# Attention of an encoder on one core: the softmax pipeline rearranged over ScalarE, VectorE, GpSimd and TensorE

## The chip, the cores and the metric

The kernel runs on one core of one Trainium2 chip. The metric is device time of the whole kernel in microseconds (us). The engines are named as in the profile: PE (TensorE matmul), PEld (TensorE weight load), DVE (VectorE), ACT (ScalarE), POOL (GpSimd), SP (SyncE, which issues the loads).

## The reference, cut to what matters

A two-layer encoder over 16 + 1024 = 1040 tokens of width 1024. Layer 0 has a mixer of a Fourier part and an attention with 6 query heads and 2 key/value heads of width 128; layer 1 has a gated recurrence; each layer has an MLP of width 4096. The change lies in the attention alone:

```
s = jnp.einsum('bqhgd,bkhd->bhgqk', qb, k).astype(jnp.float32) * scale
p = jax.nn.softmax(s, axis=-1).astype(v.dtype)
o = jnp.einsum('bhgqk,bkhd->bqhgd', p, v)
```

Every query attends to all 1040 keys, in float32.

## The kernel before, in words

Float32 products are made out of three matmuls each, with both operands split in a high part (rounded to the matmul format `fp32r`) and a low part (the rest): high x high, high x low, low x high. So `qh`/`ql`, `kh`/`kl`, `pth`/`ptl`, `vth`/`vtl` are the high and low parts of queries, keys, turned probabilities and values.

The tokens are padded to T = 1044 = 9 x 116 = 3 x 348. A **tile** is 116 queries of one query head against all 1044 keys. A **group** is three tiles (348 queries) of one head, and there are 18 groups, so 54 tiles. Tile number b * 6 + s is made by `attend(b, s)`, which stands once in the stream of each engine; b runs over 0..9 (a loop for 1..8, written out for 0 and 9) and s over 0..5. Each engine runs its own copy in its own order, and semaphores tie them: `begun` and `drained` switch off the parts of a step for which no tile exists yet or any more. For tile g (numbered from 0), in `attend` number g:

- PE: nine score matmuls into PSUM banks 0, 1, 2, one bank for 348 keys (L1942). For the first tile of a group it first waits for the low part of the group's queries (`a_ql`). Before the first matmul it waits until the exponential of tile g-1 is done (`a_exp`), since that has read the three banks. Then a third of the V products of an older group (27 matmuls for a group, 9 in each step, L1956), into bank 6 or 7. Then it turns the normalized probabilities of tile g-1 (nine transposes, three for each of the banks 3, 4, 5, L1969), and before each bank it waits for the low part that was made from that bank's old content (`a_pl`).
- DVE: low part of turned third 0 of tile g-2 (L1356), then the maximum of each score bank (L1365, three), two small instructions that make the bias of the exponential (L1367, L1370), then the low parts of thirds 1 and 2, in s = 1 and 4 the low part of the next group's queries (`q_low`, L1349), and last the reciprocal of the sum (L1381), which waits for the exponential.
- ACT: the exponential of all 1044 columns with its sum (L807), the high part of turned third 0 of tile g-1 (L813), the multiplication by the reciprocal (L819), high parts 1 and 2, and at times the copy of a finished group's output (L825) or the high part of the next queries (L769).
- POOL has nothing to do here. It splits weights elsewhere (L596 makes the high part by a multiplication by a broadcast column of ones, L598 the low part by a subtraction). The split of the out projection's first unit is made before the attention, and that of its second once PE has begun the first.

Of the kernel before, what the change touches and what calls it, by code (L numbers as in the profile page):

```python
# [78 lines left out]
def encoder(nc, x, meta, mix_gain, ab_w_in, q_gain, k_gain, ab_w_out, c_w_in, lb_logits, o_gain,  # L79
# [3 lines left out]
    with ctx:  # L83
# [28 lines left out]
        nqsc = at("nqsc", [P, NQ, 9], F32, o_c + 1484 + 72 + 216)  # L112
        amax = at("amax", [P, 8], F32, o_c + 1484 + 72 + 432)
        e_c = o_c + 1484 + 72 + 432 + 32

# [20 lines left out]
        ptl = at("ptl", [P, 2, 9, CB], F32R, o_x + 9216 + 25088)  # L136
        prob = (at("prob0", [P, T], F32, o_x + 9216 + 50176), at("prob1", [P, T], F32, o_t + 9216))
        qh = at("qh", [P, 2, CB], F32R, o_x + 9216 + 50176 + row)
# [79 lines left out]

        c_sp, c_dve = sem("carrier_sp"), sem("carrier_dve")
        w_land = [sem("unit_landed0"), sem("unit_landed1")]  # L220
# [51 lines left out]
        a_nb = sem("exp_bias_ready")  # L272
        a_exp = sem("exp_done")
        a_rc = sem("sum_inverse_ready")
# [166 lines left out]

        def turned(r):
            return ps[0:TT, 3 + r, 0:3 * TT].rearrange("p (a b) -> p a b", b=TT)

# [143 lines left out]
        def _(pool):  # L588
# [12 lines left out]
            for u in range(2):  # L601
                split(u, u % 2, 16, first=True)
            with pool.Fori(1, U_DN[0] // 2) as i:
                for slot in range(2):
                    split(i * 2 + slot, slot, i * 16 + 16)
# [70 lines left out]
        def _(act):  # L676
# [120 lines left out]

            def attend(b, s):

                g = b * 6 + s  # L800
                if not drained(b, s, 0):

                    act.wait_ge(a_nb, g + 1)
                    if begun(b, s, 2):

                        act.wait_ge(a_t, b * 18 + (3 * s - 3))
# [3 lines left out]
                def high(r):  # L810
                    if begun(b, s, 1) and not drained(b, s, 1):
                        act.wait_ge(a_t, b * 18 + (3 * s - 2 + r))
                        A(tile_cols(pth, s - 1)[:, 3 * r:3 * r + 3, :], turned(r), ACT.Copy).then_inc(a_ph, 1)  # L813

                high(0)
                if not drained(b, s, 0):
# [3 lines left out]
                high(1)  # L820
                high(2)
                if s in (2, 5) and begun(b, s, 8):

                    act.wait_ge(a_pv, b * 2 + (s // 3 - 1))
                    A(yf[:, bass.ds(group_col(b - 1, s // 3), CB)], ps[:, 6 + s // 3, 0:CB], ACT.Copy).then_inc(a_ev, 1)  # L825
                if s in (0, 3) and not drained(b, s, 0):

                    q_high(b + s // 3, 1 - s // 3)

            for s in range(6):  # L830
                attend(0, s)
            with act.Fori(1, 9) as b:
                for s in range(6):
                    attend(b, s)
            for s in range(6):
                attend(9, s)

# [306 lines left out]
        def _(dve):  # L1144
# [200 lines left out]

            def q_low(b, gg):
                dve.wait_ge(a_qh, b * 2 + (gg + 1))
                nc.vector.sem_inc(c_dve, 1)
                V.tensor_tensor(ql[:, gg, :], yf[:, bass.ds(group_col(b, gg), CB)], qh[:, gg, :], ALU.subtract).then_inc(a_ql, 1)  # L1349

            def attend(b, s):
                def low(r):
                    if begun(b, s, 2) and not drained(b, s, 2):
                        hi, lo = tile_cols(pth, s - 2), tile_cols(ptl, s - 2)
                        dve.wait_ge(a_ph, b * 18 + (3 * s - 5 + r))
                        V.tensor_tensor(lo[:, 3 * r:3 * r + 3, :], turned(r), hi[:, 3 * r:3 * r + 3, :], ALU.subtract).then_inc(a_pl, 1)  # L1356

                low(0)
                if not drained(b, s, 0):


                    col = [amax[0:TT, c:c + 1] for c in range(8)]
# [16 lines left out]
                if not drained(b, s, 0):  # L1379
                    dve.wait_ge(a_exp, b * 6 + (s + 1))  # L1380
                    V.reciprocal(col[6], col[5]).then_inc(a_rc, 1)  # L1381


            V.memset(ps[0:TT, 2, CB - (T - TOK):CB], MASKED)
            q_low(0, 0)
            qk_scale(7)
# [4 lines left out]
            for s in range(6):  # L1391
                attend(0, s)
            with dve.Fori(1, 9) as b:
                for s in range(6):
                    attend(b, s)
            for s in range(6):
                attend(9, s)

# [369 lines left out]
        def _(pe):  # L1768
# [160 lines left out]

            def attend(b, s):  # L1930

                gg, i = s // 3, s % 3
                if not drained(b, s, 0):
                    if i == 0:
                        pe.wait_ge(a_ql, b * 2 + (gg + 1))
                    if begun(b, s, 1):

                        pe.wait_ge(a_exp, b * 6 + s)
                    for c in range(3):
                        n = CB if c < 2 else CB - (T - TOK)  # L1940
                        for q, k in ((qh, kh), (qh, kl), (ql, kh)):
                            ins = M(ps[0:TT, c, 0:n], q[:, gg, i * TT:(i + 1) * TT], k[:, gg, c * CB:c * CB + n],  # L1942
                                    start=(q is qh and k is kh), stop=(q is ql))
                        ins.then_inc(a_s, 1)

                p = (s - 2) % 3
                if begun(b, s, 5 + p) and not drained(b, s, 5 + p - 2):
                    jg, jb = ((s - 5 - p) // 3) % 2, (s - 5 - p) // 6
                    if p == 0:
                        pe.wait_ge(a_pl, b * 18 + 3 * (s - 2))  # L1950
                        if begun(b, s, 5 + 6):

                            pe.wait_ge(a_ev, (b + jb) * 2 + (jg - 1))
                    for c in range(3 * p, 3 * p + 3):
                        for v, w in ((vth, pth), (vth, ptl), (vtl, pth)):
                            ins = M(ps[:, 6 + jg, 0:CB], v[0:TT, jg * 9 + c, :], w[0:TT, jg, c, :], start=(c == 0 and v is vth and w is pth),  # L1956
                                    stop=(c == 8 and v is vtl))
                    if p == 2:
                        ins.then_inc(a_pv, 1)
                if begun(b, s, 1) and not drained(b, s, 1):  # L1960

                    pe.wait_ge(a_p, b * 6 + s)
                    if not begun(b, s, 2):
                        pe.wait_ge(av_l, 5)
                    for r in range(3):
                        if begun(b, s, 2):
                            pe.wait_ge(a_pl, b * 18 + (3 * s - 5 + r))
                        for j in range(3 * r, 3 * r + 3):
                            ins = nc.tensor.transpose(ps[0:TT, 3 + r, (j % 3) * TT:(j % 3 + 1) * TT], prob[(s - 1) % 2][0:TT, j * TT:(j + 1) * TT], ident[0:TT, 0:TT])  # L1969
                        ins.then_inc(a_t, 1)  # L1970

            for s in range(6):
                attend(0, s)
            with pe.Fori(1, 9) as b:
                for s in range(6):
                    attend(b, s)
            for s in range(6):
                attend(9, s)

# [362 lines left out]
```

## Time and profile before

| what | us |
|---|---|
| median of 3 runs (2675.21 to 2677.28) | 2677.04 |
| the profiled execution's own time | 2674.69 |
| its span in the trace | 2672.9 |
| first score matmul of the attention | 205.9 |
| end of its last V product | 443.3 |
| PE busy in the whole span | 2607.0 (98%) |

The granted clock is the share of TensorE's full clock (2.4 GHz) in a stretch: 1.00 is 2.4 GHz and 0.50 is 1.2 GHz. A timeline's row gives the start, the length, the engine, the line, the operation with its tiles, how many instructions were merged in the row, and in brackets the idle time before it and what ended it.

### The profile page before, as it was taken

The numbers are of one execution on the slowest core, as the hardware profiler recorded it, in microseconds if no ns is written. First come the engines' busy times: TensorE is split into PE (matmuls) and PEld (weight loads), VectorE is DVE, ScalarE is ACT, GpSimd is POOL, SyncE is SP. The second block draws the span as 40 slices with busy tenths as digits, with TensorE's granted clock in tenths as the row PEclk, the third lists the DMA queues.
The fourth block names the chain that finished last, engine by engine and source line by source line (L and its number), as shares of the span: only waits on it lengthen the run. The fifth ranks groups of instructions, "written<-read, shape, count | busy, mean of one in ns | idle before, by whom it ended". The sixth has DMA issues, their size and how long they took to land.

```text
span 2672.9 us, 44728 instructions
## 1 busy us (share of the span) xinstructions
PE 2607.0 (98%) x18627; PEld 2346.5 (88%) x18627; DVE 1553.9 (58%) x1843; ACT 913.3 (34%) x1496; POOL 1125.8 (42%) x599
## 2 busy tenths in 40 slices
PE   7998999999999999999999999999999999999998
PEld 7997998999999999999888888887877888788887
DVE  5398887465545433335676777778485444444444
ACT  3117886133333100013344344434243333210003
POOL 3240001347777444444232232234337878444441
PEclk9999999999999999999999999999999999999999
DMA  5110000122233322222111111112112333422221
GB/s 164 32 40 1 0 0 11 45 80 96 104 113 127 120 96 96 96 86 98 41 33 36 38 33 38 36 33 92 42 49 103 105 117 107 142 99 95 94 88 71
DMA packets 175990, 193.42 MB, mean 72 GB/s; under 512 B 7762, under 2 KB 145316, under 8 KB 175814
## 3 DMA queue, kind: packets, MB, share of 16 engines
q1 hardware_dynamic: 157238, 152.29, 17.4%
q10 hardware_dynamic: 18576, 38.55, 3.8%
q8 instruction: 138, 2.26, 0.4%
q14 instruction: 38, 0.31, 0.0%
HBM read 148.61 MB, written 42.21 MB: 71 GB/s over the span
## 4 chain that ended last, share of the span: by engine, by line
PE 83%; DVE 8%; issue 4%; ACT 3%; DMA 1%; POOL 1%; SPq 0%; ACTq 0%; DVEq 0%; POOLq 0%
PE ps L1799 53%; PE ps L2055 9%; PE ps L2052 5%; PE ps L2053 5%; PE ps L1942 3%; PE ps L2153 2%; PE ps L2121 1%; PE ps L2091 1%; DVE kk L1638 1%; DMA tmp<-hidden 1%; ACT prob L807 1%; PE ps L1888 1%; PE ps L2191 1%; ACT kk L1018 1%; DVE kk L1635 1%
## 5 line engine op out<-in xcount | busy, mean ns | idle before, releaser
L596 POOL TENSOR_TENSOR wsp<-raw,ones 128x1024 fp32r<-128x1024 f32 x140 | 275.2, 1966 | 1340.6 <-PE ps L1799 1303.5
L1799 PE MATMUL ps<-xh,wsp 128*128 128x348 f32 (+2 forms) x2624 | 622.8, 358 | 9.3 <-POOL wsp L598 6.1
L1799 PE MATMUL ps<-hh,wsp 128*128 128x348 f32 (+1 forms) x2480 | 546.2, 350 | 0.0
L1799 PEld LDWEIGHTS ps<-xh,wsp 128*128 128x128 f32 x2624 | 449.5, 189 | 54.9 <-issue 11.5
L1799 PEld LDWEIGHTS ps<-hh,wsp 128*128 128x128 f32 x2480 | 428.8, 188 | 44.1
L598 POOL TENSOR_TENSOR wsp<-raw,wsp 128x1024 fp32r<-128x1024 f32 x140 | 398.0, 2843 | 11.0
L1799 PE MATMUL ps<-xl,wsp 128*128 128x348 f32 (+2 forms) x1312 | 333.9, 351 | 0.0
L1799 PE MATMUL ps<-hl,wsp 128*128 128x348 f32 (+2 forms) x1240 | 313.9, 350 | 0.0
L1799 PEld LDWEIGHTS ps<-xl,wsp 128*128 128x128 f32 x1312 | 232.4, 189 | 24.3
L1799 PEld LDWEIGHTS ps<-hl,wsp 128*128 128x128 f32 x1240 | 218.1, 188 | 22.3
L910 ACT ACTIVATE hh<-tmp 128x1040 fp32r<-128x1040 f32 (+1 forms) x64 | 68.3, 1068 | 491.5 <-DMA tmp<-hidden 369.6
L1411 DVE TENSOR_TENSOR h<-h,ps 128x1024 f32<-128x1024 f32 x80 | 97.5, 1219 | 207.9 <-PE ps L1799 202.3
L1412 DVE TENSOR_TENSOR h<-h,ps 128x1044 f32<-128x1044 f32 x72 | 89.4, 1241 | 219.4 <-PE ps L1799 217.2
L618 POOL TENSOR_TENSOR wop<-sw,wop 128x512 fp32r<-128x512 f32 x112 | 144.3, 1298 | 69.3 <-ACT wop L876 69.2
L618 POOL TENSOR_TENSOR wop<-raw,wop 128x512 fp32r<-128x512 f32 x84 | 132.4, 1576 | 68.1 <-ACT wop L876 68.1
L1460 DVE SCALAR_TENSOR_TENSOR hid<-hid,rms 128x520 f32<-128x520 f32 (+1 forms) x112 | 150.9, 1365 | 0.9
L881 ACT ACTIVATE hid<-hid 128x520 f32<-128x520 f32 (+1 forms) x112 | 71.0, 634 | 229.3 <-DVE hid L1460 229.3
L1466 DVE TENSOR_TENSOR hl<-tmp,hh 128x1040 fp32r<-128x1040 f32 (+1 forms) x64 | 122.3, 1911 | 39.5 <-ACT hh L910 39.5
L1044 ACT ACTIVATE kp<-kk 128x512 f32<-128x512 f32 x112 | 65.6, 635 | 164.0 <-PE ps L2153 145.9
L2055 PE MATMUL ps<-xh,wop 128*128 128x512 f32 x336 | 109.5, 393 | 0.0
L876 ACT ACTIVATE wop<-sw 128x512 fp32r<-128x512 f32 x112 | 70.4, 629 | 113.4 <-PE ps L2053 48.2
L608 POOL TENSOR_TENSOR sw<-sw,raw 128x512 f32<-128x512 f32 x56 | 91.3, 1631 | 2.2
(311 smaller groups left out, 4971.1 us busy)
## 6 DMA issues: line engine op xcount, KB each, us to landing
raw<-in_w SPq DMA_DIRECT2D x128, 512.0 KB, 3.9
raw<-in_c_w_in SPq DMA_DIRECT2D x40, 512.0 KB, 3.8
tmp<-hidden SPq DMA_DIRECT2D x32, 520.0 KB, 4.2
tmp<-hidden SPq DMA_DIRECT2D x32, 512.0 KB, 4.2
hidden<-hid ACTq DMA_DIRECT2D x56, 260.0 KB, 2.1
hidden<-hid ACTq DMA_DIRECT2D x56, 256.0 KB, 2.1
raw<-in_ab_w_in SPq DMA_DIRECT2D x12, 512.0 KB, 3.7
xst<-in_x SPq DMA_DIRECT2D x8, 512.0 KB, 6.5
```

Source lines behind the costliest of these rows:

```text
L596: nc.gpsimd.tensor_tensor(wsp[:, slot, 0, :], raw[:, slot, :], one, ALU.mult).then_inc(w_high, 1)
L598: nc.gpsimd.tensor_tensor(wsp[:, slot, 1, :], raw[:, slot, :], wsp[:, slot, 0, :], ALU.subtract).then_inc(w_split, 1)
L608: nc.gpsimd.tensor_tensor(a[:], left, right, op).then_inc(t_add, 1)
L618: nc.gpsimd.tensor_tensor(operand(g, 1), a, operand(g, 0), ALU.subtract).then_inc(t_low, 1)
L1411: return V.tensor_tensor(real_pieces(h[:, k, :]), real_pieces(h[:, k, :]), real_outp(s), ALU.add).then_inc(z_free, 1)
L1412: return V.tensor_tensor(pieces(h[:, k, :]), pieces(h[:, k, :]), outp(s), ALU.add).then_inc(z_free, 1)
L1460: V.scalar_tensor_tensor(hid_[b][:], hid_[b][:], 0.0, rms[:, span(layer, b % 2)], ALU.max, ALU.mult).then_inc(t_relu, 1)
L1466: V.tensor_tensor(hl[t // CH % 2][:, t % CH, where], tmp[:, t % 2, where], hh[t // CH % 2][:, t % CH, where], ALU.subtract).then_inc(l_l, 1)
L1799: ins = M(ps[:, 3 * s + c, 0:n], w(a, k), b(k)[:, c0:c0 + n], start=(k == first and a == 0 and b is xa), stop=(k == last and a == 1))
L2052: M(out[:, 0, :], left, x(k)[:, 0:width // 2], start=start, stop=stop)
L2053: ins = M(out[:, 1, :], left, x(k)[:, width // 2:width], start=start, stop=stop)
L2055: ins = M(out, left, x(k), start=start, stop=stop)
```

## The change

- The exponential is in two instructions: banks 0 and 1 (696 columns), then bank 2 (348 columns), each with a sum of its own, each with a count on `a_exp`. PE waits for the first before the scores of bank 0 and for the second before those of bank 2.
- DVE adds the two sums and then takes the reciprocal, for tile g-1 and in step g, after the two bias instructions of tile g and ahead of the low parts.
- The normalization goes from ACT (one instruction of 1044 columns) to POOL (three of 348 columns, `normalize`). `q_low` goes from DVE to POOL as well: in s = 1 and 4 it stands behind `normalize` of that tile.
- Probabilities have three buffers in place of two. PE turns tile g-2 in step g (before: g-1), high parts are of tile g-2, low parts of tile g-3 (before: g-1 and g-2), and all three low parts stand behind the bias and the reciprocal. The V products come one tile later.
- Turned tiles rotate over four banks (3 to 6) in place of three; the V products have bank 7 alone in place of 6 and 7 in turn.

POOL, behind the splits of units 0 to 12 (ql, the low part of queries, now made here):

```diff
+            def q_low(b, gg):
+
+                pool.wait_ge(a_qh, b * 2 + (gg + 1))
+                nc.gpsimd.sem_inc(c_pool, 1)
+                nc.gpsimd.tensor_tensor(ql[:, gg, :], yf[:, bass.ds(group_col(b, gg), CB)], qh[:, gg, :], ALU.subtract).then_inc(a_ql, 1)
+
+            def normalize(b, s):
+
+                pool.wait_ge(a_rc, b * 6 + (s + 1))
+                for c in range(3):
+                    part = prob[s % 3][0:TT, c * CB:(c + 1) * CB]
+                    nc.gpsimd.tensor_tensor(part, part, amax[0:TT, 9 + s % 3:10 + s % 3].to_broadcast([TT, CB]), ALU.mult).then_inc(a_p, 1)
+                if s in (1, 4):
+                    q_low(b + s // 4, 1 - s // 4)
```

ACT, the exponential and the normalization that it loses:

```diff
-                    A(prob[s % 2][0:TT, :].rearrange("p (a b) -> p a b", b=CB), ps[0:TT, 0:3, 0:CB], ACT.Exp, bias=amax[0:TT, 4:5],
-                      scale=scale_of(qsc, b, s), accum_out=amax[0:TT, 5:6]).then_inc(a_exp, 1)
...
-                    act.wait_ge(a_rc, g + 1)
-                    A(prob[s % 2][0:TT, :], prob[s % 2][0:TT, :], ACT.Copy, scale=amax[0:TT, 6:7]).then_inc(a_p, 1)
...
+                    A(prob[s % 3][0:TT, 0:2 * CB].rearrange("p (a b) -> p a b", b=CB), ps[0:TT, 0:2, 0:CB], ACT.Exp, bias=amax[0:TT, 4:5],
+                      scale=scale_of(qsc, b, s), accum_out=amax[0:TT, 5 + s % 2:6 + s % 2]).then_inc(a_exp, 1)
+                    A(prob[s % 3][0:TT, 2 * CB:T], ps[0:TT, 2, 0:CB], ACT.Exp, bias=amax[0:TT, 4:5],
+                      scale=scale_of(qsc, b, s), accum_out=amax[0:TT, 7 + s % 2:8 + s % 2]).then_inc(a_exp, 1)
```

DVE, behind the two bias instructions of the tile:

```diff
-                low(1)
-                low(2)
-                if s in (1, 4) and not drained(b, s, 0):
-                    q_low(b + s // 4, 1 - s // 4)
+                if begun(b, s, 1) and not drained(b, s, 1):
+                    left, right = (amax[0:TT, c + (s - 1) % 2:c + (s - 1) % 2 + 1] for c in (5, 7))
+                    dve.wait_ge(a_exp, b * 12 + 2 * s)
+                    V.tensor_tensor(left, left, right, ALU.add).then_inc(a_sm, 1)
+                    dve.wait_ge(a_sm, b * 6 + s)
+                    if begun(b, s, 4):
+                        dve.wait_ge(a_p, b * 18 + (3 * s - 9))
+                    V.reciprocal(amax[0:TT, 9 + (s - 1) % 3:10 + (s - 1) % 3], left).then_inc(a_rc, 1)
+                if begun(b, s, 3) and not drained(b, s, 3):
+                    hi, lo = tile_cols(pth, s - 3), tile_cols(ptl, s - 3)
+                    for r in range(3):
+                        dve.wait_ge(a_ph, b * 18 + (3 * s - 8 + r))
+                        V.tensor_tensor(lo[:, 3 * r:3 * r + 3, :], turned(odd, s - 1, r), hi[:, 3 * r:3 * r + 3, :], ALU.subtract).then_inc(a_pl, 1)
```

PE, the score blocks (the wait for `a_ql` stays as it was) and the transposes:

```diff
-                    if begun(b, s, 1):
-
-                        pe.wait_ge(a_exp, b * 6 + s)
                     for c in range(3):
+                        if c != 1 and begun(b, s, 1):
+                            pe.wait_ge(a_exp, b * 12 + (2 * s - (1 if c == 0 else 0)))
...
                     for r in range(3):
-                        if begun(b, s, 2):
-                            pe.wait_ge(a_pl, b * 18 + (3 * s - 5 + r))
+                        pe.wait_ge(a_p, b * 18 + (3 * s - 5 + r))
+                        if begun(b, s, 4) or (s == 3 and r):
+                            pe.wait_ge(a_pl, b * 18 + (3 * s - 9 + r))
```

## Rows read from the trace of the kernel before

**Rows 1.** Busy time by stretch: us, then each engine's busy time, granted clock, DMA.
```profile
205.90:443.30 237.40, 223.27 (x1460) 205.81 (x1458) 189.82 (x514) 200.01 (x362) 0.00 (x0) 0.98 0.00 0
```

**Rows 2.** The longest waits for ACT in 237.2 to 410.9 us: total, times, longest.
```profile
PEld ps L1942 <- ACT prob L807: 13.4, 42, 0.4
```

**Rows 3.** Timeline of one tile in the steady state, and the next tile's start.
```profile
301.97 0.18 PEld L1942 LDWEIGHTS ps<-kh,qh 128*116 128x116 f32 x1 [0.30 <-ACT prob L807]
...
302.75 1.47 DVE L1365 TENSOR_REDUCE amax<-ps 116x1 f32<-116x348 f32 x3
...
304.13 0.21 DVE L1367 SCALAR_TENSOR_TENSOR amax<-amax,nqsc 116x1 f32<-116x1 f32 x1
...
304.37 0.22 DVE L1370 SCALAR_TENSOR_TENSOR amax<-amax,nqsc 116x1 f32<-116x1 f32 x1
...
304.51 0.94 DVE L1356 TENSOR_TENSOR ptl<-ps,pth 116x348 fp32r<-116x348 f32 x2
...
304.73 1.22 ACT L807 ACTIVATE prob<-ps,amax,qsc 116x1044 f32<-116x1044 f32 x1 [0.32 <-DVE amax L1370]
...
304.77 1.01 PEld L1969 LDWEIGHTS ps<-ident,prob 116*116 116x116 f32 x9
...
305.85 0.19 ACT L807 ACTIVATION_READ_ACCUMULATOR prob<-ps,amax,qsc 116x1 f32 x1
...
306.09 0.18 PEld L1942 LDWEIGHTS ps<-kh,qh 128*116 128x116 f32 x1 [0.30 <-ACT prob L807]
```

**Rows 4.** Timeline of step 3, before there are V products.
```profile
226.10 0.94 DVE L1356 TENSOR_TENSOR ptl<-ps,pth 116x348 fp32r<-116x348 f32 x2
...
226.66 0.71 PEld L1969 LDWEIGHTS ps<-ident,prob 116*116 116x116 f32 x6 [1.42 <-DVE ptl L1356]
```

**Rows 5.** POOL's instructions by line: shortest, median, longest ns.
```profile
L596 POOL TENSOR_TENSOR wsp<-raw,ones x140: 1887/1896/2910, 18.8 to 2630.5; 128x1024 fp32r<-128x1024 f32 x140
...
L598 POOL TENSOR_TENSOR wsp<-raw,wsp x140: 2382/2737/3295, 20.7 to 2632.5; 128x1024 fp32r<-128x1024 f32 x140
...
L618 POOL TENSOR_TENSOR wop<-sw,wop x112: 1281/1292/1512, 585.7 to 2279.6; 128x512 fp32r<-128x512 f32 x112
```

**Rows 6.** Timeline of POOL, one weight unit.
```profile
68.48 1.90 POOL L596 TENSOR_TENSOR wsp<-raw,ones 128x1024 fp32r<-128x1024 f32 x1 [10.94 <-PE ps L1799]
70.45 2.40 POOL L598 TENSOR_TENSOR wsp<-raw,wsp 128x1024 fp32r<-128x1024 f32 x1
```

**Rows 7.** The chain that ended last: score blocks of tiles 5 and 51.
```profile
231.69 1.66 PE ps L1942 x9
...
422.09 1.69 PE ps L1942 x9
```

**Rows 8.** Timeline of the start: tile 2, its scores and bias.
```profile
218.07 0.64 PE L1942 MATMUL ps<-kh,qh 128*116 128x348 f32 x1 [0.67 <-ACT prob L807]
...
221.81 0.22 DVE L1370 SCALAR_TENSOR_TENSOR amax<-amax,nqsc 116x1 f32<-116x1 f32 x1
```

**Rows 9.** Timeline of PE after idle stretches.
```profile
446.49 0.71 PE L1799 MATMUL ps<-mh,wsp 128*128 128x348 f32 x3 [3.04 <-DVE ml L1405]
...
875.03 0.71 PE L2091 MATMUL ps<-hh,wsp 128*128 128x348 f32 x3 [2.00 <-issue]
```

**Rows 10.** Busy time by stretch behind them, the granted clock third from the end.
```profile
447.00:449.00 2.00, 2.00 (x11) 2.00 (x10) 2.00 (x2) 2.00 (x3) 1.97 (x1) 0.63 0.00 0
449.00:451.00 2.00, 2.00 (x9) 2.00 (x8) 2.00 (x2) 2.00 (x3) 1.92 (x2) 0.52 0.00 0
...
875.00:877.00 2.00, 1.97 (x13) 2.00 (x14) 0.54 (x1) 0.00 (x0) 2.00 (x2) 1.00 0.00 0
```

**Rows 11.** One DVE line by itself: shortest, median, longest ns.
```profile
L1269 DVE SCALAR_TENSOR_TENSOR rot<-tmp,small,sint x8: 1299/2842/3349, 112.0 to 203.1; 64x1044 f32<-64x1044 f32 x8
```

**Rows 12.** Timeline of POOL and DVE together.
```profile
191.63 3.28 POOL L598 TENSOR_TENSOR wsp<-raw,wsp 128x1024 fp32r<-128x1024 f32 x1
192.69 3.32 DVE L1275 SCALAR_TENSOR_TENSOR tmp<-tmp,small,cost 128x1044 f32<-128x1044 f32 x1
```

More of the change, by code:

```diff
@@ L272, in encoder @@
         a_nb = sem("exp_bias_ready")
-        a_exp = sem("exp_done")
+        a_exp = sem("exp_part_done")
+        a_sm = sem("exp_sum_ready")
+        a_pad = sem("score_pads_masked")
         a_rc = sem("sum_inverse_ready")
@@ L602, in _ @@
                 split(u, u % 2, 16, first=True)
-            with pool.Fori(1, U_DN[0] // 2) as i:
+            with pool.Fori(1, U_OUT0 // 2) as i:
+                for slot in range(2):
+                    split(i * 2 + slot, slot, i * 16 + 16)
+            split(U_OUT0, 0, 8 * U_OUT0 + 16)
+            def q_low(b, gg):
[9 more added lines that the diff above has]
+                    q_low(b + s // 4, 1 - s // 4)
+            q_low(0, 0)
+            for s in range(6):
+                normalize(0, s)
+            with pool.Fori(1, 9) as b:
+                for s in range(6):
+                    normalize(b, s)
+            split(U_OUT0 + 1, 1, 8 * U_OUT0 + 16)
+            with pool.Fori(U_OUT0 // 2 + 1, U_DN[0] // 2) as i:
                 for slot in range(2):
@@ L822, in attend @@
                 if s in (2, 5) and begun(b, s, 8):
                     act.wait_ge(a_pv, b * 2 + (s // 3 - 1))
-                    A(yf[:, bass.ds(group_col(b - 1, s // 3), CB)], ps[:, 6 + s // 3, 0:CB], ACT.Copy).then_inc(a_ev, 1)
+                    nc.scalar.sem_inc(c_act, 1)
+                    A(yf[:, bass.ds(group_col(b - 1, s // 3), CB)], ps[:, 7, 0:CB], ACT.Copy).then_inc(a_ev, 1)
+                for r in range(3):
+                    if begun(b, s, 2) and not drained(b, s, 2):
+                        act.wait_ge(a_t, b * 18 + (3 * s - 5 + r))
+                        A(tile_cols(pth, s - 2)[:, 3 * r:3 * r + 3, :], turned(odd, s, r), ACT.Copy).then_inc(a_ph, 1)
@@ L830, in _ @@
             for s in range(6):
-                attend(0, s)
-            with act.Fori(1, 9) as b:
+                attend(0, s, 0)
+            with act.Fori(0, 4) as i:
                 for s in range(6):
-                    attend(b, s)
+                    attend(i * 2 + 1, s, 1)
+                for s in range(6):
+                    attend(i * 2 + 2, s, 0)
             for s in range(6):
-                attend(9, s)
+                attend(9, s, 1)
             for k in range(8):
@@ L1344, in _, with attend @@
             qk_turn(7)
[L1346 to L1358, printed above, removed]
+            def attend(b, s, odd):
                 if not drained(b, s, 0):
-                    col = [amax[0:TT, c:c + 1] for c in range(8)]
+                    col = [amax[0:TT, c:c + 1] for c in range(5)]
                     for c in range(3):
@@ L1378, in attend @@
                         v_low(g)
[L1379 to L1385, printed above, removed]
+            V.memset(ps[0:TT, 2, CB - (T - TOK):CB], MASKED).then_inc(a_pad, 1)
             qk_scale(7)
@@ L1391, in _ @@
             for s in range(6):
-                attend(0, s)
-            with dve.Fori(1, 9) as b:
+                attend(0, s, 0)
+            with dve.Fori(0, 4) as i:
                 for s in range(6):
-                    attend(b, s)
+                    attend(i * 2 + 1, s, 1)
+                for s in range(6):
+                    attend(i * 2 + 2, s, 0)
             for s in range(6):
-                attend(9, s)
+                attend(9, s, 1)
             for k in range(8):
@@ L1959, in attend @@
                         ins.then_inc(a_pv, 1)
-                if begun(b, s, 1) and not drained(b, s, 1):
-                    pe.wait_ge(a_p, b * 6 + s)
-                    if not begun(b, s, 2):
+                if begun(b, s, 2) and not drained(b, s, 2):
+                    if not begun(b, s, 3):
                         pe.wait_ge(av_l, 5)
                     for r in range(3):
-                        if begun(b, s, 2):
-                            pe.wait_ge(a_pl, b * 18 + (3 * s - 5 + r))
+                        pe.wait_ge(a_p, b * 18 + (3 * s - 5 + r))
+                        if begun(b, s, 4) or (s == 3 and r):
+                            pe.wait_ge(a_pl, b * 18 + (3 * s - 9 + r))
                         for j in range(3 * r, 3 * r + 3):
-                            ins = nc.tensor.transpose(ps[0:TT, 3 + r, (j % 3) * TT:(j % 3 + 1) * TT], prob[(s - 1) % 2][0:TT, j * TT:(j + 1) * TT], ident[0:TT, 0:TT])
+                            ins = nc.tensor.transpose(ps[0:TT, turn_bank(odd, s, r), (j % 3) * TT:(j % 3 + 1) * TT], prob[(s - 2) % 3][0:TT, j * TT:(j + 1) * TT], ident[0:TT, 0:TT])
                         ins.then_inc(a_t, 1)
+            pe.wait_ge(a_pad, 1)
             for s in range(6):
-                attend(0, s)
-            with pe.Fori(1, 9) as b:
+                attend(0, s, 0)
+            with pe.Fori(0, 4) as i:
                 for s in range(6):
-                    attend(b, s)
+                    attend(i * 2 + 1, s, 1)
+                for s in range(6):
+                    attend(i * 2 + 2, s, 0)
             for s in range(6):
-                attend(9, s)
+                attend(9, s, 1)
             def m_ready(k):
```

47 lines of the change are left out of this document (21 added, 26 removed).

## The prediction

> **What bounds the kernel now.** I read the page first: PE is busy 98% of the span, so only a stretch in which PE idles can give time. Then the busy time by stretch. The attention runs from 205.9 to 443.3 us, 237.4 us of which PE is busy 223.3 [rows 1]; nothing outside it is touched. The waits say what PE idles for: 13.4 us over 42 steady tiles, 0.32 a tile, all for the exponential [rows 2]. The chain's score blocks give the pace: tiles 5 and 51 start at 231.69 and 422.09, so a tile takes 190.40 / 46 = 4.14 us [rows 7].
>
> The timeline of one tile shows why [rows 3]. Call T the moment at which PE loads the first score weights (301.97). At T+0.78 DVE begins the three maxima, at T+2.16 and T+2.40 it makes the bias (L1367, L1370), at T+2.76 the exponential begins, at T+4.07 its sum is out and at T+4.12 the next tile begins. PE's own work is shorter: its nine transposes start at T+2.80 and their weights take 1.01, so it is done at T+3.81. The loop scores, maxima, bias, exponential is 0.3 longer than PE's work. That 0.3 is all there is to win: 53 x 0.32 = 17 us.
>
> **The change part by part.**
>
> *The exponential in two.* Its time to the sum's readout is 1.31 (304.73 to 306.04). The first part has 696 of 1044 columns, so about a third of 1.22, 0.41, drops out; scores of bank 0 may begin at T+2.76+0.90+0.05 = T+3.71. That is before PE is free at T+3.81, so this wait is gone. The second sum costs one more readout of 0.19 on ACT, which loses the 1.16 to 1.2 of the normalization: free. The second part ends about T+4.2; bank 2 is wanted some 0.94 after the next T (six matmuls of 0.156, by 2.80 / 18), so that is free too.
>
> *DVE's order.* Here the next wait stands. The transposes of third r = 1 and r = 2 in step g need low parts 0 and 1 of tile g-3, since four banks hold only one third more than a tile. All three low parts now stand behind L1370, the addition and the reciprocal of the same step. Before, low part 0 was made early in the step and only 1 and 2 behind L1370. That this wait costs PE when the low parts are late is seen in step 3, which has no V products ahead of the transposes: PE sat idle for 1.42 and went on at 226.66, 0.04 after the low part of 226.10 was written (two take 0.94, one 0.52) [rows 4]. Now the sum: L1370 at T+2.40; +0.14 to the next DVE instruction (the addition), as from 304.37 to 304.51; +0.24 to the reciprocal, which waits for the addition as L1370 does for L1367 (304.13 to 304.37); +0.12 to the first low part, my estimate from that 0.14; +0.94 for two low parts; +0.04; then three of nine transposes, 1.01 / 3 = 0.34 [rows 3, 4]. T to T is 2.40+0.14+0.24+0.12+0.94+0.04+0.34 = 4.22. So the gain of 0.3 is used up and 0.08 is lost. Bounds: 4.14 (the pieces overlap more than I think) and 4.45 (each small instruction waits as long as it lasts, 0.21 to 0.24 more).
>
> *The low part of the queries on POOL.* Of everything that moves this is the dearest. The first scores of a group wait for `a_ql`. For the group that begins with tile 3 the count comes from `q_low`, which stands behind `normalize` of tile 1. That waits for the reciprocal of tile 1, and DVE makes it in step 2, behind L1370 of tile 2. So between L1370 of tile 2 and the scores of tile 3 there are now, in series: addition, reciprocal, three multiplications, one subtraction. The query's high part was ready long before; only the order on POOL's queue makes it late. Tiles 4 and 6 stand in the same relation, so each of the 17 group borders has it. Behind the waiting scores everything on PE queues: V products and transposes of that step don't need the queries and wait all the same.
>
> Prices on POOL: no row shows 348 columns. A subtraction of 512 columns takes 1.28 at best and one of 1024 takes 2.38 [rows 5], so 2.15 ns a column and 0.18 fixed: 0.93 for 348. The multiplication by a broadcast column takes 1.89 for 1024 [rows 5]; with the same 0.18 fixed that is 0.76 for 348, and 0.07 lies between two instructions (68.48 to 70.45 less 1.90) [rows 6]. The chain on POOL is 3 x 0.83 + 0.93 = 3.42. Lower bound, in pure proportion to columns: 3 x 0.71 + 0.81 = 2.94. Upper bound, the longest subtraction (3.295 for 1024 [rows 5]) in proportion for all: 3 x 1.19 + 1.12 = 4.69. I take 3.42, as the shapes are those of the shortest rows.
>
> At a border T to T is 2.40 + 0.14 + 0.24 + 0.16 (reciprocal and wake-up, estimated from the 0.14 and 0.04 above) + 3.42 + 0.05 + 0.10 (POOL's own wake-up, an estimate) = 6.51, from 6.0 to 7.8. A plain tile would have been 4.22, so PE idles 2.3 more there.
>
> *The rest.* `normalize` of tile g-2 ends at about T+5.6 of step g-1, and PE wants it at T+2.8 of step g, 4.22+2.8 = 7.0: hidden. POOL is free at the borders when its next set comes. A single V bank has to be copied by ACT before the next group's first product: that copy comes behind the exponential in step 2 or 5, and the next product a step later: hidden, but for the drain. Weight splits of the out projection: the second one waited for PE before and does now.
>
> *The sum*, against the profiled execution (2674.69; the median of the runs is 2.35 higher). Start: tile 2 comes at 217.3, 0.8 earlier than 218.07, by two shortened exponentials; from scores to L1370 takes 3.74 there [rows 8], at the lower clock; plus 6.51-2.40 = 4.11 gives tile 3 at 225.1. Sixteen groups of 2 x 4.22 + 6.51 = 14.95 bring tile 51 to 225.1 + 239.2 = 464.3, against 422.09 [rows 7]: +42.2. Two more tiles: +0.2. Drain: before, 13.0 from tile 53's scores (430.3) to the end at 443.3. Now one more step: 4.2 for step 53, 2 x (1.4 + 1.0) for nine V products and nine transposes each, 1.4 for step 56, 0.6 for the copy that empties the V bank, 27 products of 0.156 = 4.2, and about 0.5 of low parts that PE waits for: 15.7, so +2.7. In all +45.1: 2677.0 + 45.1 = 2722.
>
> **The rivals.**
>
> *TensorE's clock falls at each border.* After 3.04 us of idle time the granted clock was 0.63 and 0.52 in the next 4 us; after 2.00 us of idle time it stayed 1.00 [rows 9, 10]. The new idle stretch of 2.3 lies nearer to the latter. If it falls, each border loses what those rows lost, 2 x 0.37 + 2 x 0.48 = 1.7, and 17 borders 29: 2751. It decides from an idle stretch between 2.0 and 3.0.
>
> *DVE and POOL hold each other up.* A DVE instruction with two SBUF inputs took 1.30 by itself and up to 3.35 [rows 11], and beside such a one POOL's subtraction took 3.28 in place of 2.38 [rows 5, 12]. L1367, L1370 and the new addition have two such inputs. At T+2.16 POOL would still be at work only if its set of three lasted over 3.2; I expect it done by T+1.4. If it does overlap, L1367 waits for up to one multiplication (0.76), on the chain of each of the 36 plain tiles: +15 to +27, 2737 to 2749. The Trainium skill (SBUF — State Buffer, Who interferes with whom) says that such an instruction and a GpSimd one that reads SBUF exclude each other for an instruction's whole length; by that rule too the cost comes only where the two meet, and the trace agrees (3.28 against 2.38). The low parts have one input in PSUM and would be outside of it by that page.
>
> *The other side: the queries' low part is in time.* If `q_low` were ready before T+3.8 and low parts too, PE alone would set the pace: 53 x 0.32 less the drain's 2.7, 2663. Nothing before speaks for it: POOL's chain alone would have to be under 0.7 where its shortest bound is 2.94. It turns to a gain once a border costs less than 12.42 - 2 x 4.22 = 3.98.
>
> *The low parts come in time, the borders don't:* 4.14 or less for plain tiles and 6.0 at borders: 16 x 14.3 in place of 239.2, so 10 less: 2711.
>
> **How the numbers follow.** The forecast 0.60; the clock falls at most borders 0.20; DVE and POOL collide 0.08; plain tiles and borders both at the low bound 0.06; the far side 0.04, of which some lands in between. The range reaches from 2708 (the low bounds and a shorter drain) to 2756 (the clock case and some of POOL's upper bound). A change of 0.2%, 5.4 us, is about what can be told from none; only the far side and a part of the low bound could come under it: faster 0.03, same 0.02, slower 0.95.
>
> **What would show it.** In the profile after: PE's score weights idle for POOL's `ql` 17 times, about 2.3 us each and some 39 us in all; transposes wait for `ptl` in plain tiles for about 0.4; no wait of scores for the exponential; POOL rows of 0.76 and 0.93 us; a tile pace of 4.22 inside a group and 6.5 across a border; granted clock 1.00 in the attention but for its start. It would be wrong if POOL's instructions of 348 columns were far from these prices, if the clock fell, or if the wait for the low parts were hidden by something that I have put at the wrong place.

## The result: 47 us slower, by the waits at the group borders

The changed kernel takes 2723.57 us (median of 4 runs, 2723.37 to 2725.22) against 2676.12 for the kernel before in the same comparison: a ratio of 1.0178, 95% interval 1.0165 to 1.019. Its profiled execution has a span of 2721.6, 48.7 more than before.

The waits of the changed kernel in 237 to 460 us (total, times, longest) name the new one, POOL's `ql`, and no longer the exponential:

```profile
POOL prob L625 <- DVE amax L1396: 110.1, 44, 4.5
...
PEld ps L1966 <- issue: 30.2, 15, 2.0
PE ps L1966 <- POOL ql L618: 26.8, 15, 1.8
PEld ps L1993 <- issue: 10.2, 34, 2.1
```

The timeline from the end of one group to the second tile of the next, with L1966 the scores, L1388 the second bias instruction, L1392 the addition, L1396 the reciprocal, L1401 the low parts, L625 the multiplications, L618 the low part of the queries, L1993 the transposes:

```profile
299.83 0.22 DVE L1388 SCALAR_TENSOR_TENSOR amax<-amax,nqsc 116x1 f32<-116x1 f32 x1
...
299.96 0.15 DVE L1392 TENSOR_TENSOR amax<-amax 116x1 f32<-116x1 f32 x1
...
300.15 0.16 DVE L1396 RECIPROCAL amax<-amax 116x1 f32<-116x1 f32 x1
...
300.23 1.35 DVE L1401 TENSOR_TENSOR ptl<-ps,pth 116x348 fp32r<-116x348 f32 x3
300.39 2.21 POOL L625 TENSOR_TENSOR prob<-prob,amax 116x348 f32<-116x348 f32 x3 [1.89 <-DVE amax L1396]
...
302.57 0.92 POOL L618 TENSOR_TENSOR ql<-y,qh 128x348 fp32r<-128x348 f32 x1
303.61 0.18 PEld L1966 LDWEIGHTS ps<-kh,qh 128*116 128x116 f32 x1 [2.04 <-issue]
...
306.01 0.22 DVE L1388 SCALAR_TENSOR_TENSOR amax<-amax,nqsc 116x1 f32<-116x1 f32 x1
...
306.53 1.38 DVE L1401 TENSOR_TENSOR ptl<-ps,pth 116x348 fp32r<-116x348 f32 x3
...
307.11 0.71 PEld L1993 LDWEIGHTS ps<-ident,prob 116*116 116x116 f32 x6 [0.31 <-DVE ptl L1401]
...
307.79 0.18 PEld L1966 LDWEIGHTS ps<-kh,qh 128*116 128x116 f32 x1
...
311.93 0.18 PEld L1966 LDWEIGHTS ps<-kh,qh 128*116 128x116 f32 x1
```

The reader is to see two things beside [rows 3]. From the bias at 299.83 to the scores at 303.61 there is one chain, handed on within 0.12 us each time, and more than four fifths of its 3.78 us are POOL's 2.21 and 0.92 us. And inside the group (307.79 to 311.93) the pace is 4.14, as before, though no score waits for an exponential: the last six transposes wait 0.31 for the low parts.

PE's timeline at the borders, and the granted clock (third from the end) behind the ones at 273.61 and 303.62:

```profile
273.61 0.41 PE L1966 MATMUL ps<-kh,qh 128*116 128x348 f32 x1 [1.83 <-POOL ql L618]
289.23 0.41 PE L1966 MATMUL ps<-kh,qh 128*116 128x348 f32 x1 [1.79 <-POOL ql L618]
303.62 0.41 PE L1966 MATMUL ps<-kh,qh 128*116 128x348 f32 x1 [1.83 <-POOL ql L618]
318.12 0.42 PE L1966 MATMUL ps<-kh,qh 128*116 128x348 f32 x1 [1.78 <-POOL ql L618]
```
```profile
275.60:277.60 2.00, 2.00 (x8) 2.00 (x8) 1.59 (x7) 0.88 (x2) 0.33 (x1) 0.50 0.01 4
...
305.60:307.60 2.00, 1.91 (x15) 1.52 (x14) 1.84 (x8) 1.15 (x3) 0.93 (x2) 1.00 0.00 0
```

A group takes 14.4 to 14.6 us (289.23 to 303.62, 303.62 to 318.12), but 15.6 where the clock fell to 0.50 (273.61 to 289.23). Idle time of 1.83 stands ahead of both kinds. The first window lies in the slow group, the second in a fast one.

### The profile page after: what moved, and what is told of

Same layout as the page of the kernel before. It is cut to its first block, busy times and chain, and to the rows that moved or that the text cites. A ratio compares the mean times of both kernels' runs of the same rounds, so it can differ in the third digit from the quotient of the medians.

```text
span 2721.6 us, 45373 instructions
## 1 busy us (share of the span) xinstructions
PE 2623.0 (96%) x18627; PEld 2358.3 (87%) x18627; DVE 1552.3 (57%) x1878; ACT 873.9 (32%) x1550; POOL 1263.8 (46%) x780
## 4 chain that ended last, share of the span: by engine, by line
PE 79%; DVE 7%; issue 6%; POOL 5%; ACT 2%; DMA 1%; SPq 0%; POOLq 0%; ACTq 0%; DVEq 0%
PE ps L1824 52%; PE ps L2082 9%; PE ps L2079 5%; PE ps L2080 5%; POOL prob L625 3%; PE ps L2180 2%; PE ps L2148 1%; PE ps L2118 1%; DVE kk L1663 1%; DMA tmp<-hidden 1%; PE ps L1913 1%; PE ps L2218 1%; ACT kk L1047 1%; DVE kk L1660 1%; POOL ql L618 1%
## 5 line engine op out<-in xcount | busy, mean ns | idle before, releaser
L625 POOL TENSOR_TENSOR prob<-prob,amax 116x348 f32<-116x348 f32 x162 | 119.6, 766 | 143.1 <-DVE amax L1396 143.1
L1383 DVE TENSOR_REDUCE amax<-ps 116x1 f32<-116x348 f32 x162 | 80.0, 520 | 85.8 <-PE ps L1966 85.7
```

The costliest lines, as they stand in the source:

```text
L625: nc.gpsimd.tensor_tensor(part, part, amax[0:TT, 9 + s % 3:10 + s % 3].to_broadcast([TT, CB]), ALU.mult).then_inc(a_p, 1)
```

## The experiments

Each is timed against the kernel before on the same chip; a ratio is to that. The times of before that go with them are 2675.8, 2675.7, 2675.8 and (e12) 2676.7.

### The place of `q_low` in POOL's queue

```diff
             def normalize(b, s):
 
+                if s in (1, 4):
+                    q_low(b + s // 4, 1 - s // 4)
                 pool.wait_ge(a_rc, b * 6 + (s + 1))
...
-                if s in (1, 4):
-                    q_low(b + s // 4, 1 - s // 4)
```

> The changed kernel with the low part of the queries made on POOL ahead of the normalization of tiles 1 and 4, not behind it. Theory (the order on POOL's queue makes the scores wait at each group border, 6.2 us from tile to tile there against 4.14): the 17 waits for ql go, the pace is 4.14 throughout, the clock stays up after the start; what stays over the kernel before is the longer drain and the start, so 2679 to 2683. Rival (GpSimd's work itself, by its port or its length, slows the borders wherever it stands): still over 2705.

Measured: 2684.43 (2678.55 to 2686.43), ratio 1.0032 (1.0019 to 1.0045). No score waits for `ql` any more; the only waits of the scores that the view names from 240 to 420 us are three for the exponential (total, times, longest):

```profile
PEld ps L1966 <- ACT prob L842: 1.0, 3, 0.4
```

39 of the 47 us are gone by moving one instruction of 0.92 us ahead of three others. Of what stays the longer drain is the largest part in the profiled execution, the fastest of the six: from the scores of tile 53 to the out projection 19.9 us, against 16.2 in the kernel before. The same instruction on DVE, at the end of steps 1 and 4:

> The changed kernel with the low part of the queries back on DVE, at the end of steps 1 and 4 (that of the first group stays on POOL). Theory (the border wait comes from the place in the queue, not from the engine): as e1_ql_first, 2679 to 2683, if DVE's 0.5 us more in two of six steps is hidden. Rival: DVE becomes late with the maxima of the next tile there, +0.5 at 17 borders, 2688.

Measured: 2683.99 (2678.26 to 2688.38), ratio 1.0028 (1.0018 to 1.0039). Which engine does it makes no difference that these runs can tell; its place does. Both medians lie 1 to 1.5 us over the range; the spread of 8 to 10 us was not expected (see the start, below).

### The clock at the borders

```diff
                     if i == 0:
+                        if begun(b, s, 1):
+                            pe.wait_ge(a_exp, b * 12 + (2 * s - 1))
+                            for _ in range(9):
+                                M(ps[0:TT, 0, 0:CB], kh[:, gg, 0:TT], kh[:, gg, 0:CB], start=True, stop=True)
                         pe.wait_ge(a_ql, b * 2 + (gg + 1))
```

> The changed kernel with nine more matmuls of 348 columns on PE at each border, into score bank 0, ahead of the wait for ql, so that they lie in the idle time and the real scores overwrite them. Theory (the groups of 15.6 us between those of 14.45 are those in which the clock fell at the border): all groups take 14.45, the start climbs back to the full clock earlier, 6 to 12 us less than the changed kernel, 2712 to 2718, though PE has more to do. Rival (another cause of the long groups): unchanged or slower, 2724 or more.

Measured: 2718.15 (2715.95 to 2719.86), ratio 1.0151, at the upper end of the range. The granted clock is 1.00 from 250 to 460 us, where the changed kernel had 0.96 in the mean. The medians differ by 5.4 us, but in the profiled executions the attention alone is 10.0 us shorter (the out projection begins at 485.67 against 495.65): that is what the clock cost there, net of the added work. Behind it 6.1 us are lost again (2232.0 against 2225.9 us to the end), in code that no edit touches; more on that below. The rest of the loss is the wait itself.

### The reciprocal and the low parts

The addition and the reciprocal go behind the three low parts, in the changed kernel and together with the first edit:

```diff
-                if begun(b, s, 1) and not drained(b, s, 1):
-                    left, right = (amax[0:TT, c + (s - 1) % 2:c + (s - 1) % 2 + 1] for c in (5, 7))
...
-                    V.reciprocal(amax[0:TT, 9 + (s - 1) % 3:10 + (s - 1) % 3], left).then_inc(a_rc, 1)
                 if begun(b, s, 3) and not drained(b, s, 3):
...
+                if begun(b, s, 1) and not drained(b, s, 1):
+                    left, right = (amax[0:TT, c + (s - 1) % 2:c + (s - 1) % 2 + 1] for c in (5, 7))
...
+                    V.reciprocal(amax[0:TT, 9 + (s - 1) % 3:10 + (s - 1) % 3], left).then_inc(a_rc, 1)
```

> The changed kernel with the addition and the reciprocal behind the three low parts on DVE. Theory: the reciprocal comes 1.3 us later, which the border chain pays 17 times (7.5 in place of 6.2), while plain tiles no longer wait for the low parts and fall from 4.14 to about 3.85: 17 x 1.3 - 36 x 0.29 = +12, so 2736, and up to 2752 if the clock now falls at all borders, since PE idles 3 us there. Rival (the reciprocal isn't on either chain): no change from the changed kernel, 2724.

Measured: 2759.47 (2756.34 to 2760.06), ratio 1.0308. Slower, as the border chain says, but by 36 us over the changed kernel in place of 12 to 28. PE now idles 3.35 us at each border, and from 258 us on the clock falls at every one, where it fell at 5 of 14 in the changed kernel. A border takes 7.72 us from tile to tile in place of 6.19, not 1.3 but 1.53 more. The plain tiles gained nothing (4.1 where the clock is up). Both of these come from the first bias instruction, which lasts 0.47 in place of 0.21 here too, for the reason that e3 shows. 17 x 1.53 = 26 and nine more falls at about 1.2 each, 11, make about the 36.

> Both edits together: ql first and the reciprocal behind the low parts. Theory: with the border waits gone and the low parts ahead, only PE's own work is left, 3.83 to 3.87 from tile to tile: 53 x 0.29 = 15 off, 4 for start and drain on, so 2663 to 2668, faster than the kernel before. Rival (the normalization on POOL is then late, since the reciprocal is): a wait of the transposes for prob, 4.1 or more for a tile, 2680 or more.

Measured: 2694.79 (2690.1 to 2696.56), ratio 1.0066. My theory failed here: without the border wait and with the low parts early, the kernel is 10 us slower than e1, not 16 to 21 faster. The timeline of e3 shows why:

```profile
302.21 2.22 POOL L627 TENSOR_TENSOR prob<-prob,amax 116x348 f32<-116x348 f32 x3 [1.90 <-DVE amax L1401]
...
303.97 0.47 DVE L1385 SCALAR_TENSOR_TENSOR amax<-amax,nqsc 116x1 f32<-116x1 f32 x1
304.39 0.93 POOL L618 TENSOR_TENSOR ql<-y,qh 128x348 fp32r<-128x348 f32 x1
304.48 0.85 DVE L1388 SCALAR_TENSOR_TENSOR amax<-amax,nqsc 116x1 f32<-116x1 f32 x1
...
305.26 1.36 DVE L1393 TENSOR_TENSOR ptl<-ps,pth 116x348 fp32r<-116x348 f32 x3
305.47 0.93 ACT L840 ACTIVATE prob<-ps,amax,qsc 116x696 f32<-116x696 f32 x1 [2.05 <-DVE amax L1388]
```

A bias instruction of one column, 0.22 by itself, lasts 0.85 and ends when POOL's subtraction does (304.39 + 0.93 = 305.32). The other lasts 0.47 in place of 0.21, until POOL's multiplications end (302.21 + 2.22 = 304.43). The late reciprocal has moved POOL's work under them. Neither theory had named that, though the prediction had it as a rival: the group of three takes 13.1 us in the mean (4.1, 4.1 to 4.2, and 4.75 for the one with the subtraction). The low parts have one input in PSUM and keep their 1.36 beside POOL in all these timelines. The Trainium skill (SBUF — State Buffer, Who interferes with whom) says that a VectorE instruction with two SBUF inputs contends with a GpSimd one that reads SBUF, and that one with at most one SBUF input, outside of VectorE's 2-port modes, does not. The traces agree: 0.85 in place of 0.22 for the one kind, 1.36 as ever for the other.

> As e3_both, but with the exponential in one instruction of 1044 columns. Theory: the loop scores, maxima, bias, exponential is back at 4.12 to 4.14 from tile to tile, so 2677 to 2682; the difference to e3_both is what the split is worth. Rival (the split is worth nothing, the gain comes from ACT's freed time and the deeper pipeline): the same time as e3_both.

Measured: 2693.97 (2690.06 to 2698.02), ratio 1.0062: the same as e3_both, but not because the split is worth nothing. Two different waits happen to be equally long:

```profile
303.00 0.94 POOL L618 TENSOR_TENSOR ql<-y,qh 128x348 fp32r<-128x348 f32 x1
303.05 0.90 DVE L1383 SCALAR_TENSOR_TENSOR amax<-amax,nqsc 116x1 f32<-116x1 f32 x1
...
307.87 0.21 DVE L1383 SCALAR_TENSOR_TENSOR amax<-amax,nqsc 116x1 f32<-116x1 f32 x1
...
309.83 0.18 PEld L1962 LDWEIGHTS ps<-kh,qh 128*116 128x116 f32 x1 [0.24 <-ACT prob L840]
```

Once in a group the bias instruction meets POOL, and that tile takes 4.82 (4.75 in e3). In the other two it lasts 0.21 as by itself, and the scores wait 0.24 for the whole exponential: 4.12 to 4.13, as the theory said, where e3 has 4.11 from its delayed bias instructions. So this run could not say what the split is worth.

### One tensor input each

```diff
-                    V.scalar_tensor_tensor(col[3], col[0], col[1], scale_of(nqsc, b, s), ALU.max, ALU.mult).then_inc(a_mn, 1)
+                    V.tensor_scalar(col[3], col[0], col[1], scale_of(nqsc, b, s), ALU.max, ALU.mult).then_inc(a_mn, 1)
...
-                    V.scalar_tensor_tensor(col[4], col[2], scale_of(nqsc, b, s), col[3], ALU.mult, ALU.min).then_inc(a_nb, 1)
+                    V.tensor_scalar(col[4], col[2], scale_of(nqsc, b, s), col[3], ALU.mult, ALU.min).then_inc(a_nb, 1)
...
-                    V.tensor_tensor(left, left, right, ALU.add).then_inc(a_sm, 1)
+                    V.tensor_scalar(left, left, right, None, ALU.add).then_inc(a_sm, 1)
```

> e3_both with the two bias instructions and the addition written as tensor_scalar, so that each has one tensor input in SBUF and takes the rest as scalars. Theory (in e3_both these waited for POOL's instruction in progress: 0.46 to 0.51 in place of 0.21, and once in a group 0.85 in place of 0.22, because of their second SBUF input): they take 0.2 again beside POOL, the group of three tiles falls from 13.1 to about 11.6 us, 17 x 1.5 = 26 off 2695, so 2665 to 2672, faster than the kernel before. Rival (scalar operands meet POOL in the same way, or something else lengthens them): still 2690 or more.

Measured: 2676.41 (2676.0 to 2678.07), ratio 1.0 (0.999 to 1.0009). The second bias instruction by itself (shortest, median, longest ns), first in e8_one_input, then in e3_both:

```profile
L1388 DVE TENSOR_SCALAR amax<-amax,nqsc x54: 272/273/275, 213.1 to 429.5; 116x1 f32<-116x1 f32 x54
```
```profile
L1388 DVE SCALAR_TENSOR_TENSOR amax<-amax,nqsc x54: 218/220/860, 213.3 to 447.9; 116x1 f32<-116x1 f32 x54
```

The new form is 0.05 us longer by itself and never longer beside POOL. 18 us came back by it: the second SBUF input is what waited. The range was missed by 4 us: a tile takes 3.96, not 3.83.

```profile
303.08 0.18 PEld L1966 LDWEIGHTS ps<-kh,qh 128*116 128x116 f32 x1
...
305.90 1.18 PEld L1993 LDWEIGHTS ps<-ident,prob 116*116 116x116 f32 x9
...
307.04 0.18 PEld L1966 LDWEIGHTS ps<-kh,qh 128*116 128x116 f32 x1
```

The timeline names no wait here, yet the nine transposes take 1.18, where they took 1.01 in [rows 3]. A merged row hides short idle gaps inside it. The same stretch asked for in narrow windows gives the first two low parts, and the weight loads that begin the second and the last third:

```profile
305.74 0.51 DVE L1393 TENSOR_TENSOR ptl<-ps,pth 116x348 fp32r<-116x348 f32 x1
306.17 0.51 DVE L1393 TENSOR_TENSOR ptl<-ps,pth 116x348 fp32r<-116x348 f32 x1
...
306.37 0.13 PEld L1993 LDWEIGHTS ps<-ident,prob 116*116 116x116 f32 x1
...
306.79 0.13 PEld L1993 LDWEIGHTS ps<-ident,prob 116*116 116x116 f32 x1
```

The low parts end at 306.25 and 306.68, and each third begins 0.11 to 0.12 behind one. So the transposes still wait for the low parts, and these pace the tile: from its start at 303.08 2.66 to the first low part, 0.94 for two, 0.11, and 0.25 for the last three transposes make 3.96. My 3.83 took it that PE's own work was all that was left.

> e8_one_input with the exponential in one instruction. Theory: the loop with the whole exponential, 4.12 a tile, is the bound again, so 15 us over e8_one_input, 2680 to 2687: the split is worth 0.28 a tile, but only where nothing else waits. Rival: the same time as e8_one_input.

Measured: 2690.1 (2686.23 to 2691.01), ratio 1.0046 (1.0029 to 1.0062), 3 us over the range. 13.7 over e8_one_input; a tile takes 4.24 in place of 3.96. Here the split is worth the 0.28 a tile that was said, since no other wait is as long. The 4.24 are over my 4.12 since the two bias instructions in the new form are 0.05 longer each and lie on this loop.

### The split alone, in the kernel before

```diff
+                    A(prob[s % 2][0:TT, 0:2 * CB].rearrange("p (a b) -> p a b", b=CB), ps[0:TT, 0:2, 0:CB], ACT.Exp, bias=amax[0:TT, 4:5],
                       scale=scale_of(qsc, b, s), accum_out=amax[0:TT, 5:6]).then_inc(a_exp, 1)
+                    A(prob[s % 2][0:TT, 2 * CB:T], ps[0:TT, 2, 0:CB], ACT.Exp, bias=amax[0:TT, 4:5],
+                      scale=scale_of(qsc, b, s), accum_out=amax[0:TT, 7:8]).then_inc(a_exp, 1)
...
+                    V.tensor_tensor(col[5], col[5], col[7], ALU.add).then_inc(a_sm, 1)
...
+                        if c != 1 and begun(b, s, 1):
+                            pe.wait_ge(a_exp, b * 12 + (2 * s - (1 if c == 0 else 0)))
```

> The kernel before with the exponential in two parts alone (with the addition of the two sums ahead of the reciprocal). Theory: ACT then has 4.2 us of work for a tile (two exponentials, three copies, the normalization, a third of two copies more) and the reciprocal comes later, so ACT takes the place of the wait and the pace is 4.15 to 4.4: 2677 to 2691, no gain. Rival (the wait for the exponential is all that bounds the kernel before): 3.83 for a tile, 2661.

Measured: 2693.16 (2691.45 to 2693.55), ratio 1.0059 (1.0042 to 1.0076), 2 us over the range. No gain, as the theory said, but not because ACT is full:

```profile
301.45 0.93 ACT L808 ACTIVATE prob<-ps,amax,qsc 116x696 f32<-116x696 f32 x1 [0.41 <-DVE amax L1373]
...
303.13 0.16 DVE L1384 TENSOR_TENSOR amax<-amax 116x1 f32<-116x1 f32 x1 [0.96 <-ACT prob L810]
...
303.92 1.36 DVE L1368 TENSOR_REDUCE amax<-ps 116x1 f32<-116x348 f32 x3
...
305.80 0.93 ACT L808 ACTIVATE prob<-ps,amax,qsc 116x696 f32<-116x696 f32 x1
```

A tile takes 4.35 whether ACT idled 0.41 ahead of its exponential or not at all. The loop is another: DVE waits 0.96 for the sum of the second exponential, then come the addition, the reciprocal and one low part, and only behind them the maxima of the next tile, which begin 1.4 after its scores in place of 0.78 [rows 3]. So the split lengthens a chain through DVE's queue. This is read from the trace; no run moved the reciprocal alone. The changed kernel has the reciprocal a step later, and its maxima don't wait for it.

### The start, and the waits between the transposes

28 and 18 matmuls more fill PE's idle time ahead of tiles 1 and 2:

```diff
+                    if isinstance(b, int) and b == 0 and s in (1, 2):
+                        pe.wait_ge(av_l, 1)
+                        for _ in range(28 if s == 1 else 18):
+                            M(ps[0:TT, 3, 0:CB], kh[:, 0, 0:TT], kh[:, 0, 0:CB], start=True, stop=True)
```

> e1_ql_first with the same matmuls at the start. Theory (e1's runs, 2678.6 to 2686.4, differ by how long the clock stays low at the start): 2674 to 2679, within 3 us of each other. Rival (the spread is from elsewhere): 2678 to 2687 as before.

Measured: 2685.36 (2681.5 to 2688.24), ratio 1.0033. Theory fallen: the clock was 1.00 from 205.9 to 234 and the spread stayed. The profiled executions of e11 and e1 differ by 8.4 us, and 6.1 of these lie behind the attention (2232.1 against 2226.0 us).

> e8_one_input with 28 matmuls more on PE ahead of the scores of tile 1 and 18 ahead of those of tile 2, into a bank that nobody reads then, in idle time of 4.9 and 2 to 3 us. Theory (the idle start makes the clock fall, and how long it stays low differs between runs): the clock stays up at the start, 4 to 8 us off e8_one_input and runs that lie closer together: 2659 to 2667. Rival: the matmuls delay the first tiles, no gain.

Measured: 2676.77 (2675.01 to 2678.22), ratio 1.0002. The attention did become 5.1 us shorter: the out projection begins at 441.97 against 447.05 in e8_one_input. But what follows takes 2231.8 us (2673.8 less 441.97) against 2227.35. So the gain is lost later in the kernel, in code that no edit touches. The timeline around the start of the first MLP's down projection shows how that can be, first the kernel before, then the changed one:

```profile
872.47 1.24 DVE L1466 TENSOR_TENSOR hl<-tmp,hh 128x1040 fp32r<-128x1040 f32 x1 [2.09 <-ACT hh L910]
873.17 2.77 POOL L653 TENSOR_TENSOR wsp<-raw,wsp 128x1024 fp32r<-128x1024 f32 x1 [0.98 <-PE ps L2053]
```
```profile
922.38 2.34 POOL L687 TENSOR_TENSOR wsp<-raw,wsp 128x1024 fp32r<-128x1024 f32 x1
922.59 3.22 DVE L1491 TENSOR_TENSOR hl<-tmp,hh 128x1040 fp32r<-128x1040 f32 x1 [2.04 <-ACT hh L939]
...
927.13 1.20 PE L2118 MATMUL ps<-hh,wsp 128*128 128x348 f32 x3 [4.94 <-DVE hid L1495]
```

The same DVE instruction with two SBUF inputs takes 1.24 where it starts 0.7 ahead of POOL's, and 3.22 where it starts 0.2 behind; PE then idles 4.94 in place of 2.00 [rows 9] and the clock falls. Which comes first differs from run to run with the same code there. e8_one_input and e10 are alike at this place (both idle 4.90), but not at the same place of the second MLP, first e8_one_input, then e10:

```profile
2296.49 0.74 PE L2118 MATMUL ps<-hh,wsp 128*128 128x512 f32 x2 [1.33 <-DVE hl L1491]
```
```profile
2294.04 0.74 PE L2122 MATMUL ps<-hh,wsp 128*128 128x512 f32 x2 [3.69 <-DVE hl L1491]
```

That is 2.4 of the 4.5 us that e10 loses there, and the clock falls to 0.50 behind the longer idle stretch and not behind the shorter. The changed kernel idles 1.38 at this place, the kernel before and e11 3.69. These places can account for a few us of spread; no run isolated them.

> e10_one_input_start with one wait for the whole normalized tile ahead of its nine transposes, in place of one for each third. Theory (three waits for prob beside three for ptl stand between the transposes as sequencer instructions, which is why nine transposes take 1.18 us where they took 1.01, and a tile 3.96 where PE's own work is 3.81): the transposes come back to 1.05 to 1.1, a tile to 3.85 to 3.9, and 50 x 0.08 = 4 us less than e10_one_input_start, 2670 to 2675. Rival (the transposes wait for the low parts, or the time is lost later in the kernel): as e10_one_input_start, 2676 to 2678.

```diff
+                    pe.wait_ge(a_p, b * 18 + (3 * s - 3))
                     for r in range(3):
-                        pe.wait_ge(a_p, b * 18 + (3 * s - 5 + r))
```

Measured: 2672.98 (2671.51 to 2680.42), ratio 0.9989 (0.998 to 0.9998), the only version on the fast side, by 0.1%. In narrow windows again, the second low part, the first load of the last third, the readout of the first part's sum and the next tile's scores:

```profile
304.39 0.51 DVE L1393 TENSOR_TENSOR ptl<-ps,pth 116x348 fp32r<-116x348 f32 x1
...
304.95 0.13 PEld L1997 LDWEIGHTS ps<-ident,prob 116*116 116x116 f32 x1
305.02 0.19 ACT L840 ACTIVATION_READ_ACCUMULATOR prob<-ps,amax,qsc 116x1 f32 x1
...
305.26 0.18 PEld L1970 LDWEIGHTS ps<-kh,qh 128*116 128x116 f32 x1
```

The theory holds for the smaller part only: with one wait less in front of it a third begins 0.05 behind its low part, not 0.11 to 0.12, and the nine loads take 1.13 in place of 1.19. The rest is the rival, the wait for the low parts. A tile gains just 0.01 to 0.02 (3.95), because the next wait is there: the scores now begin 0.05 behind the readout of the first part of the exponential, as they did behind the whole one in the kernel before [rows 3]. Against the kernel before, e12 is 3.7 us faster and e10 1.0 slower, in different sessions; in the profiled executions 0.8 of their difference of 2.7 lies in the attention and the rest behind it.

## Why the prediction was right, point by point

Forecast 2722, measured 2723.6. The mechanism was right, the last few us are luck: with the measured tiles and borders at the full clock, 14.45 a group, sixteen groups come to 231.2 us, 8.0 under my 239.2, and the clock, which I had put at nothing there, added 11: 6.0 at five borders and 5.1 in the first two groups.

- **The border.** Named as the dearest part, with its chain. POOL's part was put at 3.42 and is 2.17 + 0.92 = 3.09: the multiplications of 0.77 overlap and follow each other every 0.72, where I had 0.83. A border takes 6.19 in place of 6.51 (2.41 + 0.13 + 0.19 + 0.24 + 3.09 + 0.12 and rounding). The scores wait for `ql` 17 times as forecast, but for 31.4 us in all, 1.85 each in place of 2.3. e1 and e5 show that the order on the queue is the cause.
- **Plain tiles.** Low parts pace them, as forecast, at 4.14 and not 4.22: the addition to the reciprocal is 0.19, not 0.24, and the low parts follow 0.10 later, not 0.12. From the end of a low part to the next tile it is 0.12 + 0.25, where I had 0.04 + 0.34. This was the low bound.
- **The wait for the exponential is gone.** Right, but by less than I thought. I had a third of 1.22, 0.41, drop out; the first part lasts 0.93, so 0.29 does. Its readout ends at T+3.78, not 3.66, and scores could begin at T+3.83, no earlier than PE's own T+3.81. e12 shows this wait come back as the next one.
- **The clock at the borders.** I had it as a rival and decided by idle length, 2.3 between 2.0 and 3.0. The idle time was 1.8 and the clock fell at 5 of the 14 borders from 259 us on, 1.2 us each. The rule of that step failed: idle length alone did not decide. It makes the mean group 14.88 ((467.50 - 259.20) / 14), by chance next to my 14.95. e6 shows the clock up at all of them once PE has work there.
- **The start.** Tile 3 came at 225.25, forecast 225.1. But the two groups behind it took 33.95 (225.25 to 259.20) in place of 29.9, at a clock of 0.54 from 220.4 to 234.9: I had let the clock recover at tile 3. This term was left out.
- **The drain.** From tile 51 to the out projection 28.15 (467.50 to 495.65) against 24.40 (422.09 to 446.49): +3.75, of which I had 2.9.
- **Behind the attention** nothing was to change: -0.5 us in sum, out of a loss of 2.9 up to the first MLP's down projection and a gain of 3.4 behind it. Tile 51 is 45.4 later, and 45.4 + 3.75 - 0.5 = 48.7.
- **DVE against POOL.** Rightly not counted for the changed kernel: its L1388 lasts 219 to 223 ns in all 54 tiles. e3 shows that one moved reciprocal makes it part of the bound.

## What to carry to other kernels

When work goes to another engine, follow the queue of that engine with the needed time of each result: an instruction of 0.92 us that the next stage waits for cost 39 us since it stood behind work that nobody was waiting for. A wait removed on a loop shows the next one at almost the same length (exponential, low parts, bias instructions, low parts, exponential again in these runs); before splitting an instruction, work out where its engine, the other engines and the reader's second wait stand. When a merged row of a timeline takes longer than it did and names no wait, ask for it in narrow windows: gaps of 0.1 us hide in it. And before GpSimd is set to work beside VectorE, look for tiny VectorE instructions with two SBUF inputs on the critical chain, and give them scalar operands.

## What the runs showed of the hardware that was not expected

- A DVE instruction of one column waited for the end of POOL's instruction in progress: 0.85 us in place of 0.22. `tensor_scalar` with two scalar pointers and one tensor input took 0.27 and never waited.
- After the same idle time of 1.83 us on PE the granted clock was 0.50 once and 1.00 another time.
- A transpose that waited for a low part began 0.05 us behind its end where that was its only wait (e12), and 0.11 to 0.12 behind it where one more wait, long fulfilled, stood beside it (e8).
